# A three-block network on one core: six small moves in the order of block one

## The reference

```python
h_res = jnp.concatenate([meta, x], axis=1)            # 16 meta tokens ahead
h = rmsnorm(h_res, norm_g[l])
proj = h @ w_in[l]                                    # 9 parts: glu_a, glu_b, z, q, f, i, g, m_conv, m_rec
# conformer branch
a = u_a * jax.nn.sigmoid(u_b)
c = causal depthwise convolution of a, 31 taps, + conv_b
c = jax.nn.silu(layernorm(c, ln_g, ln_b))
y_conv = (c * jax.nn.silu(z)) @ w_out
# recurrent branch, 8 heads of 128
q = jax.nn.silu(q_raw);  f = lb + (1.0 - lb) * jax.nn.sigmoid(f_raw)
k = 1.0 - f;  S_new = exp(b_last) * S + (k * exp(b_last - b))^T v     # b: running sum of log f
o = rmsnorm per head;  y_rec = (o * jax.nn.silu(g)) @ w_out
merged = jax.nn.sigmoid(m_conv) * y_conv + jax.nn.sigmoid(m_rec) * y_rec
h_res = h_res + merged @ w_out[l]
```

## Time and profile before

| What | Value |
|---|---|
| Median of three runs | 3795.52 us (3794.46 to 3797.2) |
| The profiled execution, its own time | 3796.67 us |
| Its span in the trace | 3795.4 us |
| PE busy, of the span | 3690.3 us, 97% |
| DVE, ACT, POOL busy | 1720.7, 1178.2, 1091.7 us |
| Granted TensorE clock, mean | 0.989 |

### The profile page before, as it was taken

How to read it: one execution, slowest core, us unless ns; L and a number is a source line. 1 busy time by engine, 2 the same in 40 slices (tenths; PEclk the granted TensorE clock), 3 DMA queues, 4 the chain that set the end, 5 groups by cost and what they waited for, 6 DMA issues and landing times.

```text
span 3795.4 us, 42159 instructions
## 1 busy us (share of the span) xinstructions
PE 3690.3 (97%) x17644; PEld 3015.8 (79%) x17644; DVE 1720.7 (45%) x2132; ACT 1178.2 (31%) x1523; POOL 1091.7 (29%) x747
## 2 busy tenths in 40 slices
PE   6999999999999999999999999999999999999998
PEld 6989887888878876777788888887777788888886
DVE  5665615999543472225432222225667642222226
ACT  5555423222231344443321211114322331121113
POOL 3333321222233441112432222225113342222223
PEclk9999999999999999999999999999999999999999
DMA  2011021111232341101321111113101221111112
GB/s 102 28 30 33 23 78 50 56 56 56 72 137 96 103 132 35 37 27 36 106 67 50 45 48 48 46 49 126 44 28 51 89 72 45 51 45 47 48 46 76
DMA packets 64988, 229.29 MB, mean 60 GB/s; under 512 B 7200, under 2 KB 7328, under 8 KB 64672
## 3 DMA queue, kind: packets, MB, share of 16 engines
q1 hardware_dynamic: 64800, 226.60, 18.2%
HBM read 201.40 MB, written 25.17 MB: 60 GB/s over the span
## 4 chain that ended last, share of the span: by engine, by line
PE 88%; DVE 7%; ACT 2%; issue 1%; POOL 1%; DMA 1%; SPq 0%; DVEq 0%; ACTq 0%
PE psum L505 77%; PE psum L853 2%; PE psum L617 2%; PE psum L868 2%; PE psum L883 1%; DVE work L2171 1%; PE psum L588 1%; PE psum L739 0%; POOL wl L3114 0%; PE psum L702 0%; DVE qb L2173 0%; PE psum L641 0%; PE psum L640 0%; DVE fb L2094 0%; DVE k L2828 0%
## 5 line engine op out<-in xcount | busy, mean ns | idle before, releaser
L3114 POOL TENSOR_TENSOR wl<-raw,wh 128x512 fp32r<-128x512 f32 x636 | 882.7, 1408 | 2378.3 <-ACT wh L1185 2378.3
L505 PE MATMUL psum<-hh,wh 128*128 128x512 f32 (+2 forms) x3760 | 1186.8, 391 | 38.4 <-POOL wl L3114 15.7
L505 PE MATMUL psum<-hh,wl 128*128 128x512 f32 (+2 forms) x3760 | 1150.2, 382 | 0.0
L505 PE MATMUL psum<-hl,wh 128*128 128x512 f32 (+2 forms) x3760 | 1145.3, 380 | 0.0
L505 PEld LDWEIGHTS psum<-hh,wh 128*128 128x128 f32 x3760 | 676.2, 190 | 185.4 <-issue 30.9
L505 PEld LDWEIGHTS psum<-hh,wl 128*128 128x128 f32 x3760 | 699.4, 190 | 134.5
L505 PEld LDWEIGHTS psum<-hl,wh 128*128 128x128 f32 x3760 | 698.5, 190 | 133.2
L1185 ACT ACTIVATE wh<-raw 128x1024 fp32r<-128x1024 f32 x318 | 335.1, 1054 | 791.5 <-PE psum L505 785.0
L505 PE MATMUL psum<-hdh,wh 128*128 128x512 f32 x1024 | 333.9, 398 | 5.0 <-DVE B L3015 4.4
L505 PE MATMUL psum<-hdh,wl 128*128 128x512 f32 x1024 | 331.1, 395 | 0.0
L505 PE MATMUL psum<-hdl,wh 128*128 128x512 f32 x1024 | 331.1, 396 | 0.0
(11 more groups left out here) (422 smaller groups left out, 3019.3 us busy)
## 6 DMA issues: line engine op xcount, KB each, us to landing
raw<-in_wts SPq DMA_DIRECT2D x318, 512.0 KB, 3.5
keep_x<-B SPq DMA_DIRECT2D x14, 512.0 KB, 5.8
X<-in_xin SPq DMA_DIRECT2D x8, 520.0 KB, 5.2
keep_sz<-tmp SPq DMA_DIRECT2D x8, 512.0 KB, 2.9
av<-keep_gr SPq DMA_DIRECT2D x8, 512.0 KB, 3.4
tmp<-keep_sz SPq DMA_DIRECT2D x8, 512.0 KB, 3.5
av<-keep_gc SPq DMA_DIRECT2D x8, 512.0 KB, 3.8
xc<-keep_x SPq DMA_DIRECT2D x8, 512.0 KB, 5.8
```

Source lines behind the costliest of these rows:

```text
L505: ins = pe.matmul(out, w, x[:, k, c0:c0 + width], start=first and n == 0, stop=final and n == 2)
L3114: gp.tensor_tensor(wl[:, s, a], raw[:, s, a], fp(wh[:, s, a]), SUB).then_inc(*c.lo.tick(i, p))
```

## The change

It has seven parts, all in block one:

1. SP loads the first 256 columns of `cst` (identity and ones), then the first two slabs, then the other 1904 columns. PE and DVE wait for these ahead of the CONV products.
2. ACT runs a root on one column as soon as the squares are done, ahead of the copies of slabs 0 and 1.
3. ACT evacuates head 0's `f` between the copies of slabs 2 and 3.
4. DVE issues `hgrn_kd(ahead)` behind `qe` and `right` of the last level, in seven heads.
5. PE's head norm begins two turns later (DVE's reciprocals too).
6. PE spreads the row of `cs` four turns behind its sums, where it was two.
7. `conv_gate` takes four turns a tile, where it was two, on ACT, DVE and SP, and SP issues the first three loads of the gate tiles in the last GATE_C product, ahead of the last store of `gc`.

```diff
@@ tensor
         def head_norm():
+            yield from pause(2)
             xs = [grab(aux, ("hn", j), c.cv_act("root", j)) for j in range(2)]
...
             token_sums("cs", accc)
-            yield from pause(2)
+            yield from pause(4)
             pe.wait_ge(*c.inv("cs"))
             spread("cs", 1)
 
+        pe.wait_ge(*c.loaded("cst", "rest"))
         side.add(head_norm())
@@ scalar
             se.activation(dst, X0[:, k, :], SQUARE).then_inc(*c.sq.tick("in", k))
+
+        se.wait_ge(*c.sq("in", 7))
+        se.activation(rr[:, 1, 0:1], sq0[:, 0, 0:1], SQRT)
         split(1)
         roots("in", 0, SQRT, meta=True, scale=1.0 / 1024, bias=EPS)
...
-        duo(HGRN)
+        split(HGRN + 2)
         for h in range(8):
...
             lead_and_rest("f", h, i, fb[:, s, :], ACT.Sigmoid)
+            if h == 0:
+                split(HGRN + 3)
...
                 se.activation(Cb[:, k, :], Cb[:, k, :], ACT.Silu, scale=V("ln_g", k),
                               bias=V("ln_b", k)).then_inc(*c.cv_act.tick("silu", k))
-                yield
-                yield
+                yield from pause(4)
@@ vector, hgrn
             ve.tensor_tensor(kx, kx, lev(LAST + 1), MUL)
-            yield from pause(2)
-            if ahead:
-                hgrn_kd(ahead)
             ve.wait_ge(*c.hg_act("qe", h))
             ve.tensor_tensor(qe, qe, q, MUL).then_inc(*c.hg_dve.tick("qe", h))
             ve.wait_ge(*c.hg_dve("qe", h))
             ve.tensor_tensor(q, q, lev(LAST), MUL).then_inc(*c.hg_dve.tick("right", h, LAST))
+            yield from pause(2)
+            if ahead:
+                hgrn_kd(ahead)
             yield
             keep(4)
@@ vector
         def head_norm():
-            yield from pause(8)
+            yield from pause(10)
...
-                yield
-                yield
+                yield from pause(4)
 
         side.add(head_norm())
+        ve.wait_ge(*c.loaded("cst", "rest"))
@@ sync
-        load(("cst",), cst[:, :], A["cst"])
+        load(("cst",), cst[:, 0:256], A["cst"][:, 0:256])
         fetch(1)
+        load(("cst", "rest"), cst[:, 256:], A["cst"][:, 256:])
...
+        def gate(k):
+            if k < 3:
+                sp.wait_ge(*c.acc_v("cs", 5 + k))
+            else:
+                sp.wait_ge(*c.cv_dve("cf", k - 3))
+            sp.wait_ge(*c.stored("sz", k))
+            load(("sz", k), tmp[:, (31 + k) % 3, :], SZ[k])
+
         def conv_gate():
-            for k in range(8):
-                if k < 3:
-                    sp.wait_ge(*c.acc_v("cs", 5 + k))
-                else:
-                    sp.wait_ge(*c.cv_dve("cf", k - 3))
-                sp.wait_ge(*c.stored("sz", k))
-                load(("sz", k), tmp[:, (31 + k) % 3, :], SZ[k])
-                if k > 1:
-                    yield
-                    yield
+            for k in range(3, 8):
+                yield from pause(4)
+                gate(k)
 
         for m in range(8):
             slab(GATE_C + m, last=(m == 7))
+            if m == 7:
+                for k in range(3):
+                    gate(k)
             sp.wait_ge(*c.ev("gc", m))
             store(("gc", m), GC[m], gate_buf(m))
```

## The result

The changed kernel takes 3770.8 us (median of four executions, 3768.89 to 3772.85), the kernel before 3796.01 (3794.46 to 3797.2). The ratio is 0.9933, with a 95% interval of 0.9921 to 0.9945: the change makes the kernel faster, by 0.7%. Forecast were 3773.8 and a range of 3766 to 3782. The total lies within the range, but partly for other reasons than the sum gave, and partly by luck: one term was too small by 7.9 us, and the medians show 3.6 us less than block one gave.

A forecast was written before the change was run, and what follows sets the result against it. PE, busy 97% of the span, was taken as the bound, so time could come only from its gaps and low clock. Terms 2.0 + 6.4 + 1.4 + 2.3 + 1.5 + 8.1 = 21.7 us gave 3773.8 us, range 3766 to 3782.

The forecast's parts named there:

- Opening, 2.0: Before the first product: split constants start PE's sums 0.9 earlier, early root table ends the root 0.3 behind them; 2.0 us.
- Opening evacuation, 6.4: Head 0's `f` out before PE needs it: the 3.6 us gap goes, and 2.8 of low clock behind it; 6.4 us.
- which nothing on PE needs for a whole product: Opening evacuation: slab 3's copy and `q`'s evacuation, late next at about 61.4, were taken to hold up nothing on PE.
- Heads, 1.4: Seven heads: PE's wait for `right` goes but moves to `keep(4)`'s first piece mid-level; 0.2 to 0.3 a head, 1.4 us.
- POOL's pair of slab operations comes at 223.84: Heads: POOL gets the shared port just before `kd`, which takes 2.24, so `keep(4)` starts at 226.13 as before.
- The rival with `kd` first: Heads: `kd` gets in ahead of POOL, 1.3 us a head, 9.1 in seven; total 3766.1 us, chance 16%.
- a wait for `Ab` under 0.5: Sign in PE's waits, L617 on the last level: 1.3 seven times was forecast; under 0.5 means the `kd`-first rival holds.
- Head norms, 2.3: Norms two turns later: 4.0 us saved on the first square's wait and clock, 1.7 of new gap at CONV; net 2.3.
- Spread of `cs`, 1.5: Before the spread of `cs`: PE's wait of 1.5 us is filled by two more steps; 1.5 us gained.
- Gate, 8.1: REC: PE's 5.1 us gap for slab REC+2's low part goes with 3.0 of clock loss; 8.1 us.
- Two things were late together: Gate: POOL's operations on slab REC+2 (done 1102.32) and the evacuation that frees the pair (ends 1098.62) were both late.
- rival on the slower side: REC wait stays, 3781.9 us (12%); lock bites twice in heads, 3782.6 (4%) or, with clock, 3803.6 (3%); no effect, 3792.0 (4%).

## Why the prediction was right, and where it was not

**Opening, 2.0.** 1.8 measured: 0.8 by the earlier start of the sums, and just under 1.0 behind it. The first was forecast at 0.9, but other profiles with the split start as late as 17.11, so in this execution it is partly chance. In the second, the early table was booked a share that it doesn't have: once the slabs arrive early, the table load is hidden anyway. The 2.66 us that the Trainium skill gives for a change of table (ScalarE: Activation LUTs, What ACT_TABLE_LOAD costs) play no part here either: the load stands at 14.46 to 15.74 and the next activation starts at 15.76.

**Opening evacuation, 6.4.** The mechanism is right, the size was 5.5. The gap of 3.6 and its 2.8 of clock are gone. The step that failed is "which nothing on PE needs for a whole product": I followed ACT's queue to 61.4 and stopped. One product further on `vb` is due, and it stands behind the first head's exponential: 0.66 of wait became 1.34. That makes 5.7; the remaining 0.2 is open. With the part undone it is 4.6, because the low clock cost 1.7 there and not 2.8.

**Heads, 1.4.** This term was wrong; it measured 9.3. The step: "POOL's pair of slab operations comes at 223.84, just before DVE would start `kd`, so `kd` takes 2.24 as `right` did". I took over the outcome of one contest, between `right` and POOL, for another, between `kd` and POOL, with the times unchanged. They differ in two ways. `right` waits on a semaphore of `qe`, the instruction just before it, and starts 0.03 us after that one ends; `kd` waits for nothing in flight, and starts 0.08 before `right` ends. And the times did change, by a tenth: counted from the head's first L608, POOL's pair comes at 36.53 in both kernels, but the DVE instruction ahead of the contest ends at 36.52 where it ended at 36.62. Together these put `kd` 0.09 ahead of POOL in the records, where `right` stood 0.12 behind. The Trainium skill's rule (SBUF — State Buffer, Who interferes with whom) that the order of issue decides fits these two cases by their records. It fits the run with the long memset, where `kd` won from 0.06 to 0.08 behind, only if the recorded start isn't the time of issue. Whether an instruction without a wait asks while its predecessor runs, or the records of the two engines are merely off by some 0.1 us, is open; a `kd` with an added wait on `right` would help to tell and wasn't tried. The rival with `kd` first, at 1.3 a head and 16%, had the size right to 0.03 a head, and its sign, a wait for `Ab` under 0.5, is what the list of waits shows.

**Head norms, 2.3.** 2.3 measured, 2.45 with the part undone. The new gap was foreseen at 1.7 and came at 1.54, in the place named, with the clock at 1.00.

**Spread of `cs`, 1.5.** 1.5, shown by the wait that came back.

**Gate, 8.1.** 8.4 measured, 7.4 undone: right in size, half right in cause. "Two things were late together" holds, to 0.01 us, because both hang on DVE's row of gate operations, and the spreading mends both. The early loads, by which I explained why DVE would be in time, are worth 0.3 at most.

**The total.** 21.7 forecast, 28.8 in block one: 7.9 more from the heads, 0.9 less from the evacuation. 1.3 of it went to the low clock behind one later gap in this execution; by the medians 3.6 are missing, and only one execution of each kernel has a trace to look for them in. That the median came within 3.0 us of the forecast is luck to that extent. No rival on the slower side came true: no wait in the heads is over 0.2.

## What to carry to other kernels

Don't carry the outcome of one contest for a port over to another. Here 0.2 us decided on 9 us: an instruction that waited on its own predecessor started 0.03 after its end, one that didn't 0.08 before it, and that was half of the margin. Where a reordering hangs on less than a few tenths, give both outcomes their price. When a reordering closes a gap, follow each queue that it changes on to the next evacuation that PE needs, not only to the one that was late. And try a shift of the tiles in SBUF by some bytes: here 32 bytes were worth three quarters of what the whole change gave.

## What was unexpected of the hardware

**Addresses.** Matmuls with 512 columns of `hdh` or `hdl` (in block three `hdh3`, `hdl3`) have a median of 389 ns when the tile begins at a multiple of 64 bytes and of 394 to 397 when it begins 32 beyond, in three kernels with the former and eleven with the latter, which do the same in these stages. There are 3072 of them in blocks two and three. A pair starts every 454 in place of 467 ns; 3072 x 6.5 ns is 20 us at most, and 17 to 19 were seen. Why is open. `hh` and `hl` are read from multiples of 64 and take 392 to 396, so something else has a part in it; whether other tiles that moved along matter was not tried either.

**The clock.** The same gap does not always cost the same. Behind the wait for `pp` in block two, 2.69 us in each of these kernels, the windows behind it differ. The changed kernel:

```profile
1710.00:1721.00 11.00, 10.76 (x59) 1.00 0.02 9
```

The kernel before:

```profile
1739.00:1750.00 11.00, 10.97 (x53) 0.84 0.00 0
```

The kernel with the 160-column memset:

```profile
1711.00:1722.00 11.00, 11.00 (x46) 0.69 0.00 0
```

That is 0, 1.8 and 3.4 us. Over 14 profiles, the gaps of 2.7 us at three places between 1370 and 2610 us lost nothing in 8 cases, 1.5 to 1.8 in 30, and over 3 in 4; gaps from 1.3 to 1.7 with no longer one near them never lost anything, in some eighty cases. That may be why a kernel with several long gaps varies by a few microseconds from one execution to the next, the changed kernel among them (3769.2, 3772.39, 3768.89, 3772.85); each kernel has one trace only, so it isn't shown. This is why differences of 2 to 3 us between medians (the kernel with part 3 undone, 2.3 us above after, though 4.6 behind by the marks) are read from the marks and not from the medians.

Nor does a low clock always cost time. Behind the gap of 4.6 us ahead of the first product, eight of the 14 profiles have the low clock and six don't, for example the kernel with the one-column memset and the changed kernel:

```profile
30.30:41.30 11.00, 10.12 (x42) 0.72 0.00 0
29.30:40.30 11.00, 9.15 (x42) 1.00 0.00 0
```

By window times (1 - clock) the first would have lost 3.1 us. But from the first product to head 0's L608 it takes 41.34 and the changed kernel 41.31. PE waits for POOL's `hl` there, 0.9 in place of 1.8, and the wait ends 8.2 us behind the first product in both: while PE has to wait for its operand anyway, the clock is not what counts.
